# A fused decoder step on one core: where the index key pages are loaded, and by which engine

## The reference, cut to what matters

```python
def index_scores(q_i, w_i, k_i):
    s = jnp.einsum('bqhd,bsd->bqhs', q_i, k_i)
    return jnp.einsum('bqh,bqhs->bqs', w_i, jax.nn.relu(s)) * IDX_SCALE
# samples: k_i = cache_k_idx[page_table] and the new tokens' own keys
vals, sel = lax.top_k(scores, 256)      # then attention over the keys of sel
```

## Time and profile before

| | |
|---|---|
| median of 3 runs | 2404.21 us |
| profiled execution, first to last instruction | 2493.9 us (no time around it is given) |
| TensorE / VectorE / GpSimd / ScalarE busy | 1810.2 / 1433.9 / 1307.8 / 307.8 us |
| bytes moved | 791.92 MB, of it 604.58 by GpSimd's gathers |
| mean granted clock of TensorE | 0.853 |

### The profile page before, as it was taken

One profiled execution on the slowest core, in us unless ns is written; L12 is line 12 of the kernel. 1 busy time (PEld: TensorE's weight loads), 2 busy tenths in 40 slices (PEclk: granted clock), 3 DMA queues, 4 the chain that ended last, 5 costly groups with the idle time before them and its releaser, 6 DMA issues.

```text
span 2493.9 us, 23573 instructions
## 1 busy us (share of the span) xinstructions
PE 1810.2 (73%) x7244; PEld 768.0 (31%) x7247; DVE 1433.9 (57%) x3191; ACT 307.8 (12%) x732; POOL 1307.8 (52%) x1175
## 2 busy tenths in 40 slices
PE   9999988899699635566666766776777884555566
PEld 6767646644244201111112121221223250110011
DVE  2115876898845643999856569854444437434400
ACT  0214442111011101001101010110110010000000
POOL 1100000467655744555555557766777747677664
PEclk9998987999899867777778789998999997876678
DMA  5206322999989976999999999999999999999997
GB/s 182 71 3 195 102 85 68 355 328 410 361 306 368 346 281 238 394 367 400 386 401 380 401 371 362 371 356 368 378 384 409 409 370 374 364 359 380 355 377 287
DMA packets 259648, 791.92 MB, mean 318 GB/s; under 512 B 31522, under 2 KB 56163, under 8 KB 258947
## 3 DMA queue, kind: packets, MB, share of 16 engines
q0 software_dynamic: 166400, 604.58, 63.6%
q1 hardware_dynamic: 91268, 180.82, 20.6%
q10 hardware_dynamic: 1856, 5.03, 0.5%
HBM read 784.13 MB, written 5.59 MB: 317 GB/s over the span
## 4 chain that ended last, share of the span: by engine, by line
POOL 13%; DMA 10%; PE 8%; issue 7%; SPq 7%; another core or an unknown queue 6%; DVE 2%; ACT 1%; POOLq 0%
POOL arena L918 13%; DMA arena<-v_b 4%; PE ps L1369 3%; SPq L841 3%; DMA arena<-peer_v,arena 3%; SPq L768 2%; DMA arena<-peer_u,arena 2%; PE ps L1325 2%; DMA arena<-kv_a 2%; SPq L834 1%; PE ps L1202 1%; DVE arena L2081 1%; PE ps L1302 1%; ACT arena L1640 0%
## 5 line engine op out<-in xcount | busy, mean ns | idle before, releaser
L1369 PE MATMUL ps<-arena 128*32 128x512 f32 x2304 | 767.5, 717 | 346.6 <-DMA arena<-peer_v,arena 287.9
L2081 DVE CUSTOM_DVE_ANT_0 arena<-arena 128x1024 f32<-128x1024 f32 x576 | 694.7, 1225 | 531.5 <-DMA arena<-peer_u,arena 475.7
L918 POOL DMA_INDIRECT arena<-peer_v,arena x576 | 623.4, 1082 | 445.9 <-PE ps L1369 245.0
L918 POOL DMA_INDIRECT arena<-peer_u,arena x576 | 664.1, 1153 | 311.8 <-issue 162.2
L1369 PEld LDWEIGHTS ps<-arena 128*32 128x32 f32 x2304 | 153.4, 122 | 877.7 <-issue 662.1
L1164 PE MATMUL ps<-arena 128*128 128x448 f32 (+2 forms) x512 | 156.8, 467 | 13.1 <-DVE arena L1997 12.4
L1202 PE MATMUL ps<-arena 128*128 128x384 f32 (+2 forms) x704 | 146.5, 368 | 10.0 <-ACT arena L1576 8.1
L1325 PE MATMUL ps<-arena 128*64 128x512 f32 (+1 forms) x512 | 102.6, 538 | 68.1 <-DMA arena<-v_b 57.3
L900 POOL MEMSET arena<- 128x1024 f32 x1 | 1.0, 953 | 282.4 <-ACTq L723 282.4
L950 PE MATMUL ps<-arena 128*128 128x296 f32 (+1 forms) x512 | 132.1, 419 | 6.2 <-DMA arena<-xT 6.2
L1699 ACT ACTIVATE arena<-arena 128x8 f32<-128x8 f32 x72 | 15.3, 216 | 943.1 <-PE ps L1369 635.2
(11 more groups left out here) (211 smaller groups left out, 1694.1 us busy)
## 6 DMA issues: line engine op xcount, KB each, us to landing
arena<-k_b SPq DMA_DIRECT2D x128, 256.0 KB
arena<-v_b SPq DMA_DIRECT2D x128, 256.0 KB
arena<-w_mix SPq DMA_DIRECT2D x56, 512.0 KB
arena<-w_q SPq DMA_DIRECT2D x48, 512.0 KB
arena<-kv_a SPq DMA_DIRECT2D x128, 128.0 KB
arena<-w_out SPq DMA_DIRECT2D x24, 512.0 KB
arena<-peer_u,arena POOLq DMA_INDIRECT x576
arena<-peer_v,arena POOLq DMA_INDIRECT x576
```

The source lines that it names most:

```text
L918: pool.indirect_dma_start(out=rows[slot_of[n]], out_offset=None, in_=io["peer_v"] if v else io["peer_u"], in_offset=bass.IndirectOffsetOnA ...
L1369: last = pe.matmul(bank(6 + a, 512, 32 * lane, 32 * lane + 32), strips[:, GT * (G % 2) + k % GT, MID - r_:MID - r_ + 32], rows[slot_of[n]] ...
L2081: dve.tensor_tensor_reduce(out=row, in0=row, in1=h, scale=1.0, scalar=0.0, op0=ALU.mult, op1=ALU.add, accum_out=pre[:, k:k + 1]).then_inc( ...
```

## The change

The keys' blocks of four pages get a function, `key_pages`, and are divided: chunk 0 goes in pairs of pages behind the 16 query weights of merge 1 on SP; chunk 1 and the first half of chunk 3 stay on SP behind merge 1; chunk 2 and the second half of chunk 3 are issued by ScalarE, in 12 items of the plan, two gathers apart, that begin one gather after the first index product's place. The places of the index products and of the groups' steps move: the gaps before the first group are 64 gathers instead of 79, and the last four of the groups get one gather more in each of four steps.

```diff
@@ -488,6 +488,9 @@
         GROUP0 = [sum(GROUPS[:i]) for i in range(5)]
 
 
+        SP_KEYS = ((1, range(NB)), (3, range(NB // 2)))
+        ACT_KEYS = [(2, b) for b in range(NB)] + [(3, b) for b in range(NB // 2, NB)]
+
         due = [[] for _ in range(NG + 1)]
         where = {}
 
@@ -514,9 +517,9 @@
             return out
 
         def sample_items():
-            out = [(("zero",), 0), (("spread", 0), 1), (("ix", 0), 3), (("iy", 0), 34), (("ix", 1), 12)]
+            out = [(("zero",), 0), (("spread", 0), 1), (("ix", 0), 6), (("iy", 0), 22), (("ix", 1), 6)]
             for c in range(2, 5):
-                out += [(("ix", c), 2), (("iy", c - 1), 14 if c == 2 else 3)]
+                out += [(("ix", c), 4), (("iy", c - 1), 8 if c == 2 else 3)]
             out += [(("iy", 4), 2), (("admit",), 1)]
             out += [(("s_score", 0, c), 5) for c in range(5)]
             out += [(("s_max", 0), 2), (("s_exp", 0), 2), (("s_norm", 0), 2), (("s_turn", 0), 3)]
@@ -533,8 +536,9 @@
                     if q + 1 < NB:
                         out += [(("s_score", q + 1, c), 3) for c in range(5)]
                 if q + 1 < NB:
-                    out += [(("s_max", q + 1), 2)] + ([(("s_out", q), 1)] if q < 3 else [])
-                    out += [(("s_exp", q + 1), 2), (("s_norm", q + 1), 2), (("s_turn", q + 1), 3)]
+                    e = 1 if q >= 3 else 0
+                    out += [(("s_max", q + 1), 2 + e)] + ([(("s_out", q), 1)] if q < 3 else [])
+                    out += [(("s_exp", q + 1), 2 + e), (("s_norm", q + 1), 2 + e), (("s_turn", q + 1), 3 + e)]
             return out
 
         in_prompt = [("turn", 0), ("score", 0, 0)] + [("query", 0, m) for m in range(4)]
@@ -557,6 +561,8 @@
         put(where["route", 1, 3, 3] + 2, "gate_in", 1)
         put(where["route", 1, 3, 3] + 5, "gate", 1)
         at = s_start = m1_end + 2
+        for j, (c, b) in enumerate(ACT_KEYS):
+            put(s_start + 2 + 2 * j, "keys", c, b)
         q_at_ = {}
         for item, gap in sample_items():
             put(at, *item)
@@ -709,6 +715,15 @@
                 return out_read, KD * p + m + 1
             return qp_ready, 2 * PH * p + m + 1
 
+        def key_block(c, b, j):
+
+            p0, at = 64 * (b % 2), b // 2 * 512 + j * 128
+            return ring[c][p0:p0 + 64, at:at + 128]
+
+        def key_page(no):
+
+            return io["kidx"].rearrange("(n d) k -> n d k", d=64)[bass.ds(no, 1)].rearrange("o d k -> (o d) k")
+
         def token_of(i, k):
 
             return 32 * (k % LANES[i]) + k // LANES[i]
@@ -794,10 +809,20 @@
                 t0, nt = MTILES[i]
                 sp.dma_start(hrow[i][0:nt, :], io["x"][t0:t0 + nt, :]).then_inc(xr_loaded[i], 16)
 
+            def key_pages(c, b, j0, n):
+                nos = page_numbers(b * NPG + 4 * c + j0, n)
+                for j, no in enumerate(nos, j0):
+                    sp.dma_start(key_block(c, b, j), key_page(no)).then_inc(ring_loaded[c], 16)
+
             def first_merges():
                 sp.dma_start(subk[:], io["subk"]).then_inc(subk_loaded, 16)
                 for w in range(first_query + 2 * NMW, first_of_last):
                     weights(w)
+                    if merge_weights[w][:2] == ("query", 1):
+                        m = merge_weights[w][2]
+                        if m == 0:
+                            sp.wait_ge(mix_done, KD)
+                        key_pages(0, m // 2, 2 * (m % 2), 2)
                     if w in (52, 56, 60):
                         x_rows(w // 4 - 12)
                     if w == 64:
@@ -809,18 +834,10 @@
 
             def sample():
 
-                for c in range(4):
-                    if c:
-                        sp.wait_ge(sc_ready, 13 + c)
-                    else:
-                        sp.wait_ge(mix_done, KD)
-                    for b in range(NB):
-                        nos = page_numbers(b * NPG + 4 * c, 4)
-                        p0, at = 64 * (b % 2), b // 2 * 512
-                        for j, no in enumerate(nos):
-                            sp.dma_start(ring[c][p0:p0 + 64, at + j * 128:at + (j + 1) * 128],
-                                         io["kidx"].rearrange("(n d) k -> n d k", d=64)[bass.ds(no, 1)].rearrange(
-                                             "o d k -> (o d) k")).then_inc(ring_loaded[c], 16)
+                for c, bs in SP_KEYS:
+                    sp.wait_ge(sc_ready, 13 + c)
+                    for b in bs:
+                        key_pages(c, b, 0, 4)
                 for z, (kind, q, c, e) in enumerate(fill_list):
                     s_ = z % NSLOT
                     if kind == "ki":
@@ -1595,6 +1612,15 @@
                     act.wait_ge(coef_ready, 4 * (i - 1) + g + 1)
                 act.activation(gl[:, 32 * g:k1], pre[:, 32 * g:k1], ACT.Gelu).then_inc(gelu_done, 1)
 
+            def keys(c, b):
+
+                act.wait_ge(sc_ready, 13 + c)
+                at = b * NPG + 4 * c
+                nos = nc.values_load_multi_w_load_instructions(
+                    pages[0:1, at:at + 4], engines=(mybir.EngineType.Activation,), min_val=0, max_val=NPOOL - 1)[1]
+                for j, no in enumerate(nos):
+                    act.dma_start(key_block(c, b, j), key_page(no)).then_inc(ring_loaded[c], 16)
+
             def index_relu(c):
                 w = 512 if c < 4 else SN
                 for g in range(2):
@@ -1724,6 +1750,8 @@
                     gate_exp(*at)
                 elif kind == "gelu":
                     gelu(*at)
+                elif kind == "keys":
+                    keys(*at)
                 elif kind == "ix":
                     index_relu(*at)
                 elif kind == "iy":
```

## The result

The changed kernel takes 2416.32 us (median of 12 runs, 2405.21 to 2425.40) against 2402.90 (12 runs, 2394.87 to 2410.39) for the kernel before in the same series: a ratio of 1.0054, with 1.0036 to 1.0073 as its 95% interval. It is 13 us slower, where 25 us less had been forecast. Its profiled span is 2420.2 us, in a run of 2422.2. A ratio compares only the runs within 1.5% of the fastest of their kernel, which drops none here and about half of the kernel before's on the slow chips further down.

What follows compares the result with a forecast made beforehand. Row gathers and page loads bound the second half, with DMA idle only where SP issues index pages late. -37 (hole) + 12 (ScalarE's blocks) + 0 + 0 = -25 us, 2404 to 2379; own range 2366 to 2392, 8 in 10 2360 to 2406.

Steps and rivals of the forecast that it cites:

- -37 (hole): From 880 to 1000 us, DMA share 0.72 while products wait for index pages; closing this saves 37 us.
- the gap of 89.7 us: Profiled span 2493.9 against the runs' median 2404.21; the profiled execution was taken as slower and the difference carried over.
- Rival A: Pages bound by transfers, or issuing quicker unprofiled and the hole largely the profile's: 0 to -10 us, 2399; chance 0.25.
- Later groups. Value 0, bounds -6 and +2: Sample part's later groups and last merge: merge one gather later, +1.4 us at most; wider steps answer waits; value 0.
- The first and second chunk: Index key pages: first hidden in SP's idle time among query weights, 0 (-3.4 to +3.4); second meets its product, 0.
- "+12" for ScalarE's blocks: Relu behind ScalarE's twelve page blocks comes at 909.5, holds TensorE 24 us; GpSimd stops 9 to 16, taken as 12.
- the 6.0 taken: Time in us for one ScalarE block of four index key pages, taken nearest to SP's slow chunk.
- the low bound of 4.65: SP's price in us without a hitch for a block of four pages; at it GpSimd doesn't stop.
- Rival B: ScalarE's page blocks are dear: from 8.05 us each the change loses, at 10 net +23, 2427; chance 0.10.

Runs made afterwards that it cites:

- b_again: The kernel before without an edit, profiled a second time, on chip 5: 2400.05 us, ratio 0.9992, profiled span 2400.0 us.
- early_home2: The change with index products and first four groups at the old places, later groups and last merge as changed; slow chip 6: 2475.00 us, 1.0034 to the kernel before.
- early_home3: The change with the index products' old gaps, later groups and last merge as changed; chip 2: 2417.80 us, 1.0070 to the kernel before.
- phase1: The kernel before with only its last merge begun one gather later (765); chip 4: 2409.45 us, 1.0039 to the kernel before.
- split_only: The kernel before with only the keys divided, all places as before; chip 5: 2401.08 us, 1.0004 to the kernel before.
- no_late: The change without the wider steps, last merge 15 gathers before its old place; chip 5: 2414.33 us, 1.0049 to the kernel before.
- groups_home3: The change with all groups and the last merge at old places, only index products closer; chip 2: 2407.52 us, 1.0024 to the kernel before.
- late_home2: The change with the last four groups and last merge at their old places; slow chip 6: 2474.09 us, 1.0012 to the kernel before.
- after_again: The changed kernel, unchanged, run again on slow chip 6: 2489.65 us, 1.0050 to the kernel before.

## Why the prediction was wrong

**The step that failed first is the term "-37 (hole)".** The arithmetic was right for the execution profiled and its cause was named rightly. But that execution was of the slow kind (its chip isn't on record; its rates are, see the last section), and the forecast subtracted its hole from a median of runs that take 2403. b_again, profiled at their speed, has no such hole. The prediction saw the gap of 89.7 us and carried it over as a constant. It was the sign that the term did not apply. Rival A (0.25) named this and computed the ends of the issuing within 3 us, though its time, 2399, misses the loss as well. The objection made to it, that no other hole of that kind was in the trace, proves nothing, since only here does a product wait for a long chain of issues. On a slow chip the size of the term is borne out: early_home2 is 33 us ahead at gather 300. A small slip beside it: of the 54.6 us, 51.2 us in two pieces lie in the window named, 3.4 before it.

**The second is "Later groups. Value 0, bounds -6 and +2".** The measured term is +13 us, since the division alone is 1.0004 (some 5 us less if the closer products cost something, see below; early_home3, with the later places and not the closer products, has +17). It was priced as a shift of one gather, 1.4 us. What counts is which instruction a wait finds ahead of it: the one gather alone is +7.5 us (phase1 against the kernel before), a hold with 15 us of TensorE at half its clock behind it, and the last four groups at earlier gathers go with twice the page waits. The wider steps were to shorten TensorE's waits for ScalarE at the transposes, 19.9 us in eight pieces. After, in 1010 to 2400 us:

```profile
PE ps L1319 <- ACT arena L1666: 19.5, 7, 7.9
```

Without the wider steps it is 14.5 us in b_again, 21.9 in split_only and 25.8 in no_late, so nothing clear was gained.

**The first and second chunk: right.** The query weights hid the first chunk: share 0.90 against 0.89 and 0.88 in b_again, no product waits for them, and split_only is neutral. From 640 to 785 us SP waited 88.7 us for query products, in b_again 114.0: the pages were issued in SP's idle time.

```profile
SPq L780 <- PE ps L1219: 88.7, 12, 37.1
```

**"+12" for ScalarE's blocks: not there.** ScalarE and SP in the kernel after:

```profile
830.46 2.48 ACTq L1622 DMA_DIRECT2D arena<-kidx  x4
835.01 7.09 ACTq L1622 DMA_DIRECT2D arena<-kidx  x8
844.13 39.34 ACTq L1622 DMA_DIRECT2D arena<-kidx  x36
883.58 1.09 ACT L1630 ACTIVATE arena<-ps 128x512 f32<-128x512 f32 x2 [40.84 <-issue]
```

```profile
821.64 53.04 SPq L815 DMA_DIRECT2D arena<-kidx  x48
```

Twelve blocks from 830.5 to 883.5 us are 4.4 us each, below the 6.0 taken and even below the low bound of 4.65. The relu comes at 883.6 and not at 909.5, TensorE is not held, and GpSimd's longest stop from 820 to 930 us is 3.0 us instead of 9 to 16:

```profile
POOL arena L935 <- PE ps L1386: 17.9, 11, 3.0
```

Rival B named the wrong mechanism for the right sign. No rival had the slower side through the places.

**What stays open.** groups_home3, with only the index products closer, is at 1.0024 and split_only at 1.0004; the intervals overlap and the chips differ, so whether the closer products cost some 5 us isn't settled. The parts don't add up: early_home3 is at 1.0070 and the whole change at 1.0054, though the intervals overlap. Why the page waits double with the last four groups at earlier gathers, and what they cost, was not tried; nor was the division alone on a slow chip. No version beat the kernel before on the quick chips; late_home2 has the lowest time on a slow one, 12 us under the kernel before by the medians, but its ratio's interval holds 1.

## What to carry to other kernels

Before a hole in a profile is priced, compare the profiled span with the times of the runs. Where they differ by more than the scatter of the runs (here 3.7%), ask of every term whether it belongs to that execution alone, and take those with issue or transfer rates in them as suspects. In a written order in which two kinds of items alternate, a shift by one place is not a shift by one item's time: look up what each wait finds ahead of it at the new place, try shifts of one and of two, and look at the granted clock behind a hold as well as at the hold. And a step that makes room for a second one, as the divided keys did, is to be timed without the second.

## What the runs showed of the hardware

The same kernel takes 2401 to 2402 us on three chips (5, 2 and 4) and 2485 to 2486 on two others (13 and 6), 3.5% apart. On the quick kind SP issues 32 pages with numbers read at run time in 34.7 us, on the slow kind in 43.3 to 48.6 (first profile); ScalarE takes 4.4 and 7.1 us for a block of four. Issuing from both side by side didn't slow SP on the quick kind (48 pages in 53.0 us, the change); on the slow kind 32 pages then took SP 64.8 us (after_again). The row gathers go with it, in windows of the kernel before, first profile and b_again:

```profile
2100.00:2360.00 260.00, 128.43 (x490) 26.22 (x490) 113.65 (x267) 8.34 (x23) 182.84 (x184) 0.74 0.98 370
```

```profile
2100.00:2360.00 260.00, 151.39 (x553) 33.08 (x549) 85.74 (x142) 9.03 (x27) 195.85 (x205) 0.76 1.03 409
```

There is no hole in either. GpSimd's 184 gathers against 205 in the same 260 us are 1.41 against 1.27 us for one. This stage tells the kinds apart: the gathers from 900 to 1151 take 319.0 to 320.0 us in all eleven traces of the quick kind, 358.2 to 361.4 in the eight from chips 13 and 6, and 361.3 in the first profile, which is why that one is counted as slow.

The slower rate doesn't hold everywhere. Of the 99 us by which the first profile is behind b_again at the last gather, 45 are lost by gather 300, the hole among them, only 13 from 300 to 900, and 42 from there on.

A stop of TensorE cost more than its length in these places. After 5.2 us without work its granted clock was 0.50 for 15 us (phase1, from 1860 us), and in the change 0.50 for 15 us after 7.5 us without work (from 1890 us), with the DMA share at 0.83 and 0.87.
